# Seven products for eight over all eight input tiles of the up-projections of a two-block transformer kernel

## The reference

```python
def sq_relu_mlp(u, w_up, w_down):
    hdn = jax.nn.relu(u @ w_up)        # (1024, 1024) @ (1024, 4096)
    return (hdn * hdn) @ w_down        # (1024, 4096) @ (4096, 1024)
```

## Time and profile before

| | |
|---|---|
| median of 3 runs | 2346.39 us |
| the profiled execution | 2347.34 us, of which 2344.1 us is the span of its instructions |
| TensorE busy | 2322.2 us, 99% of the span, 11044 matmuls |
| VectorE (DVE), GpSimd (POOL), ScalarE (ACT) busy | 64%, 46%, 31% |
| DMA | 123.31 MB, 53 GB/s on average |

### The profile page before, as it was taken

How to read it: one execution, slowest core, us unless ns; L and a number is a source line. 1 busy time by engine, 2 the same in 40 slices (tenths; PEclk the granted TensorE clock), 3 DMA queues, 4 the chain that set the end, 5 groups by cost and what they waited for, 6 DMA issues and landing times.

```text
span 2344.1 us, 31876 instructions
## 1 busy us (share of the span) xinstructions
PE 2322.2 (99%) x11044; PEld 1939.3 (83%) x11044; DVE 1493.2 (64%) x2090; ACT 724.5 (31%) x1175; POOL 1084.9 (46%) x1218
## 2 busy tenths in 40 slices
PE   8999999999999999999999999999999999999997
PEld 6888888888888888888888888888888888888886
DVE  6666667756567666765566656554676676677434
ACT  4233333323434433343330002002343344333411
POOL 4332323334556565655443333544465565656432
PEclk9999999999999999999999999999999999999999
DMA  4111101022111112111112111111111111121112
GB/s 152 37 29 36 35 28 36 28 90 72 54 55 54 45 54 63 49 50 54 55 45 72 37 37 45 45 45 45 45 46 59 58 54 45 54 63 46 54 54 81
DMA packets 37525, 123.31 MB, mean 53 GB/s; under 512 B 4800, under 2 KB 5952, under 8 KB 37440
## 3 DMA queue, kind: packets, MB, share of 16 engines
q1 hardware_dynamic: 36432, 120.54, 16.7%
q10 hardware_dynamic: 1008, 1.62, 0.2%
HBM read 117.95 MB, written 4.19 MB: 52 GB/s over the span
## 4 chain that ended last, share of the span: by engine, by line
PE 96%; DVE 2%; DVEq 1%; issue 0%; DMA 0%; SPq 0%; ACT 0%
PE prod_ps L583 13%; PE prod_ps L585 13%; PE prod_ps L584 13%; PE prod_ps L842 6%; PE prod_ps L841 6%; PE prod_ps L840 6%; PE side_ps L842 5%; PE side_ps L841 5%; PE side_ps L840 5%; PE prod_ps L926 4%; PE prod_ps L925 4%; PE prod_ps L927 4%; PE side_ps L720 2%; PE side_ps L636 2%; PE side_ps L642 1%; PE side_ps L926 1%
## 5 line engine op out<-in xcount | busy, mean ns | idle before, releaser
L583 PE MATMUL prod_ps<-operand_hi,w_hi 128*128 128x512 f32 x1464 | 584.1, 399 | 4.9 <-DVE operand_lo L1183 2.8
L585 PE MATMUL prod_ps<-operand_hi,w_lo 128*128 128x512 f32 x1464 | 572.5, 391 | 0.0
L584 PE MATMUL prod_ps<-operand_lo,w_hi 128*128 128x512 f32 x1464 | 571.5, 390 | 0.0
L452 POOL CAST w_hi<-w_raw 128x1024 fp32r<-128x1024 f32 x86 | 92.4, 1074 | 701.3 <-PE prod_ps L585 680.4
L486 POOL TENSOR_TENSOR w_lo<-w_raw,w_hi 128x256 fp32r<-128x256 f32 x160 | 143.9, 918 | 405.8 <-ACT w_hi L2192 405.8
L456 POOL TENSOR_TENSOR w_lo<-w_raw,w_hi 128x256 fp32r<-128x256 f32 x344 | 327.3, 981 | 6.9
L583 PEld LDWEIGHTS prod_ps<-operand_hi,w_hi 128*128 128x128 f32 x1464 | 275.5, 188 | 63.6 <-issue 4.8
L585 PEld LDWEIGHTS prod_ps<-operand_hi,w_lo 128*128 128x128 f32 x1464 | 275.3, 188 | 58.8
L584 PEld LDWEIGHTS prod_ps<-operand_lo,w_hi 128*128 128x128 f32 x1464 | 275.9, 188 | 53.1
L925 PE MATMUL prod_ps<-operand_hi,w_hi 128*128 128x512 f32 x384 | 149.9, 390 | 0.0
L926 PE MATMUL prod_ps<-operand_lo,w_hi 128*128 128x512 f32 x384 | 149.8, 390 | 0.0
(11 more groups left out here) (308 smaller groups left out, 4844.3 us busy)
## 6 DMA issues: line engine op xcount, KB each, us to landing
w_raw<-stream SPq DMA_DIRECT2D x202, 512.0 KB, 3.5
x_in<-x_t SPq DMA_DIRECT2D x16, 256.0 KB, 6.1
x_res<-x_t SPq DMA_DIRECT2D x8, 512.0 KB, 4.6
out_t<-x_res SPq DMA_DIRECT2D x16, 256.0 KB, 2.1
w_raw<-stream SPq DMA_DIRECT2D x8, 128.0 KB, 4.8
masks_f<-masks SPq DMA_DIRECT2D x1, 896.0 KB, 7.9
ret_rows<-head_rows ACTq DMA_DIRECT2D x1, 512.0 KB, 3.7
ret_cos<-rope ACTq DMA_DIRECT2D x1, 512.0 KB, 4.5
```

The lines of the kernel that those rows point to most:

```text
L583: nc.tensor.matmul(into, w_h, a_h, start=(k == 0), stop=False)
L584: nc.tensor.matmul(into, w_h, a_l, start=False, stop=False)
L585: last = nc.tensor.matmul(into, w_l, a_h, start=False, stop=(k == KT - 1))
```

## The change

The up pairs (all but the first of each perceptron) use seven products for eight over all eight input tiles: tiles 4 to 7 get their own operands (`y_op`, with T1 to T4) and their own pair unit, in slot 1. Each of the seven products is then two wino halves, slot 0 by `x_op` and slot 1 by `y_op`. `upper` and its bank b_z go. The order in a pair becomes P1, P5, P6, P2, P7, P3, P4.

There is no room for T2, T3 and T4 of tiles 4 to 7, so they share their place with residual tiles 0 to 5 (`swapped`): the residual tiles are written to DRAM (`park_x`) and read back (`fetch_x`), and the operands are read again (`fetch_op`), in every group.

The weights of both slots are prepared before an up pair: `split_both` on GpSimd, `both_first_highs` and `both_last_highs` on ScalarE, and on DVE the sums of S3 and S4 of both slots stand ahead of the addition and Relu of c12. The core of the diff, shortened:

```diff
-                def up_pair(g, r, q, u, into, start=False, ...
+                def up_pair(g, r, q, u, into, both_split=True, new=False, behind_down=False, fetched=False, in_last=None):
...
+                    copied(g, r, 1)
+                    bank = b_u
+                    both(S2, T2, False, 3, y_wait=1).then_inc(up_prod, 1)
+                    bank = b_w
+                    both(A12, B21, True, None).then_inc(up_prod, 1)
+                    copied(g, r, 3)
...
+                def squares_late(g, r, u, h, b, then=None, between=None):
+                    act.wait_ge(evac, at(g, 16, 2 * (u0 + u) + 2))
+                    nc.scalar.activation(h[2], h[2], ACT.Square).then_inc(h_sq, 1)
+                    if then is not None:
+                        then(2)
+                    if between is not None:
+                        between()
+                    relu_copy(g, r, u, h, b)
+                    act.wait_ge(evac, at(g, 16, 2 * (u0 + u) + 4))
+                    nc.scalar.activation(h[1], h[1], ACT.Square).then_inc(h_sq, 1)
...
+                def both_last_highs(g, q, u):
+                    for slot in range(2):
+                        high_s34(slot, summed(g, q, 3 + slot))
+                    for slot in range(2):
+                        unit_free(g, u + slot)
+                        high_a22(slot)
...
-                    squares_early(g, 3, far_h)
-                    highs(g, 8, 12, 0)
-                    squares_late(g, 3, 10, far_h, far_banks)
+                    both_first_highs(g, 3, 11, 12)
+                    squares_early(g, 3, far_h)
+                    squares_late(g, 3, 10, far_h, far_banks, between=lambda: both_last_highs(g, 11, 12))
...
-                    finish_up(g, 3, 10, far_banks, far_h, before12=lambda: all_sums(g, 12, 0))
+                    finish_up(g, 3, 10, far_banks, far_h, sums_behind(g, 3, 12, 1),
+                              before12=lambda: more_sums_behind(g, 3), before11=sums_behind(g, 3, 12, 0))
...
+                finish_up(g, 3, 10, far_banks, plain_h(2), lambda: sum_then_lows(WINO_GROUPS - 1, 3, 12, 0, near_h),
+                          before21=lambda: more_sums_behind(WINO_GROUPS - 1, 3), before11=sums_behind(g, 3, 12, 0))
...
+                for op, m, half in ((B11, 4, 0), (B12, 4, 1), (B21, 6, 0)):
+                    for kk in range(2):
+                        part = nc.scalar.activation(y_raw[op][:, kk], x_res[:, m + kk, tokens(half)], ACT.Copy,
+                                                    scale=gain[:, gain_row, m + kk:m + kk + 1])
+                    part.then_inc(y_scaled, 1)
```

More of the change, by code:

```diff
@@ new lines, in up_pair, with half, both @@
+                def up_pair(g, r, q, u, into, both_split=True, new=False, behind_down=False, fetched=False, in_last=None):
+                    b_u, b_v, b_w = into[:3]
+                    u += u0
+                    def half(bank, slot, which, op, first, part, y_wait=None):
+                        if part is not None:
+                            if both_split:
+                                parts(g, q, 2 * part - 1 + slot)
+                            else:
+                                parts(g, q + slot, part)
+                        if slot and y_wait is not None:
+                            if new:
+                                pe.wait_ge(y_ready, 4 * index + (2, 1, 3, 4)[y_wait])
+                            elif fetched and y_wait:
+                                pe.wait_ge(op_back[y_wait - 1], at(g, 16, 16 * (first_group + 1)))
+                        return wino(bank, slot, which, (x_op, y_op)[slot][op], first and slot == 0)
+                    def both(*product, y_wait=None):
+                        half(bank, 0, *product)
+                        return half(bank, 1, *product, y_wait=y_wait)
+                    pe.wait_ge(evac, at(g, 16, 2 * u - 4))
@@ L944, in up_pair @@
                     if behind_down:
                         free(g, PAIRS - 2, "P4")
[L946 to L947 removed]
+                    half(b_u, 0, A11, B11, True, 1)
+                    if not new:
+                        half(b_u, 1, A11, B11, True, 1).then_inc(up_prod, 1)
                     pe.wait_ge(evac, at(g, 16, 2 * u - 2))
[L949 to L951 removed]
@@ L952, in up_pair @@
[L952 to L963, removed]
@@ L974, in up_pair @@
[L974 to L980, removed]
+                    half(b_v, 0, S1, T1, True, 2)
@@ new lines, in up_pair @@
+                    copied(g, r, 3)
+                    bank = b_u
+                    both(S3, T3, False, 4, y_wait=2).then_inc(up_prod, 1)
+                    copied(g, r, 2)
+                    bank = b_v
+                    both(S4, B22, False, None).then_inc(up_prod, 2)
+                    pe.wait_ge(up_taken, at(g, 2, first_up + r + 1))
+                    pe.wait_ge(w_split, at(g, 8, u + 1))
+                    half(b_u, 0, A22, T4, False, None).then_inc(prod, 2)
+                    if in_last is not None:
+                        in_last()
@@ L1576, in end_c12 @@
                     def end_c12():
-                        nc.vector.tensor_tensor(c12, b_v, c21 if not last else last_u2, ALU.add)
+                        nc.vector.tensor_tensor(c12, b_v, c21, ALU.add)
                         dve.drain()
```

480 lines of the change are left out of this document (355 added, 125 removed).

## The result

The changed kernel takes 2363.46 us (median of 4 runs, 2361.13 to 2364.0) against 2346.39: a ratio of 1.0066, 95% interval 1.0054 to 1.0079. It is slower by 17 us. The forecast was 2345, with a range up to 2362; the median lies 1.5 us outside it, and on the other side of no change than my likeliest case.

What follows compares the result with a forecast made beforehand. TensorE, busy 99% of the span, was taken to bound the kernel by its number of matmuls. Terms -41.2 + 19.2 + 13.6 + 4.8 + 1.6 = -2.0 us against 2347.34 gave 2345, range 2322 to 2362.

Steps and rivals of the forecast that it cites:

- my likeliest case: The prediction's own sum of terms, 2345 us with its own range 2335 to 2355, chance 0.50.
- Matmuls: Up pairs after each perceptron's first: 180 matmuls fewer on TensorE at 0.2273 us each, a gain of 40.9 us.
- Near wait: Near pairs: TensorE waits 1.6 us for ScalarE's first copy, 12 times, 19.2 us (bounds 1.0 to 2.2 each).
- Rival 1: S3/S4 sums on DVE wait in full for GpSimd, 1.5 to 3 us: +21, 2366 us, chance 0.12.
- Plain phases: Last two pairs of each perceptron: TensorE waits 3.4 us for the copy, 4 times, 13.6 us.
- Start: Start of each perceptron: six y_raw scalings ahead of copy 1, 2.4 us wait, twice, 4.8 us (2 to 7).
- Second pair: Second up pair of each perceptron: first copy late by 0.8 us, twice, 1.6 us (0 to 4).
- First plain product: Reordered plain product: saves the 0.17 us wait ahead of it, twice, a gain of 0.3 us.
- Rivals 2 and 3: 2: near wait absent because queues run down faster, 2326, chance 0.20; 3: all new waits hidden, 2306, chance 0.08.
- Transfers: Nine DMAs of 1 MB in each group, at most 7.0 us each, costed at nothing.
- rival 4: Transfers or weights late in SyncE's queue, delaying near pairs; 2 us in 12 groups gives 2369, chance 0.10.
- some 5 us of room: Slack claimed for the tightest transfer: residual tiles 0 and 1, fetched after P6 of the near pair, before DVE needs them.

Runs made afterwards that it cites:

- The kernel with all moves: Changed kernel with c12 ahead of the far-phase sums, copies ahead of start scalings, first plain units split early, plain low parts moved: 2315.31 us, ratio 0.9866.

## Why the prediction was wrong

The mechanism was right in kind: what is saved on TensorE is given back in waits for ScalarE's copy of P1, late because `relu_copy` stands behind a longer list. The forecast was 18 us too low, and the range 1.5. Step by step, each waiting term with its 0.27 included:

- **Matmuls**: 180, 40.9 us. Right.
- **Near wait**: 1.6 forecast, 17.1 / 12 + 0.27 = 1.7 measured; 20.3 for 19.2. Right, and the undoing of the sums' place gave 22.3 back. The copy ended some 7 us behind the pair's start, as worked out. The way there was only nearly right: `relu_copy` at 3.2 and not 3.6, and GpSimd, which I put beside all four sums, ran beside the first two only and was then idle for 3.74 us, since its next low parts wait for the S3 and S4 high parts. Rival 1, sums that wait in full for GpSimd, therefore fell: the four took 2.1 us, 0.5 more than alone, where it asked for 1.5 to 3. That its time, 2366, is near the measured one is luck.
- **Plain phases**: 13.6 forecast, 11.1 measured. Fair.
- **Start**: 4.8 forecast, 5.0 measured. Right.
- **Second pair**: 1.6 forecast, 3.8 measured, inside its own bounds (0 to 4), but by another hand. GpSimd's low part of the next unit ended the wait, not the copy.
- **First plain product**: forecast as a gain of 0.3, measured as a cost of 6.0. This is the first step that failed. I counted the 0.17 us of the earlier trace rows as saved, which they were, and put the product's first matmul at nothing. Before, TensorE was done with the slot of the first plain unit 24 matmuls ahead of the end of the last pair; after, 6. GpSimd's cast and low parts, 2.77 us of waiting, can't be fitted in there. In the row below GpSimd had waited 11.50 us for that slot. I had not asked, of a reordered product, when its weights' buffer comes free.

```profile
1152.97 1.04 POOL L552 CAST w_hi<-w_raw 128x1024 fp32r<-128x1024 f32 x1 [11.50 <-PE side_ps L967]
1154.10 2.78 POOL L556 TENSOR_TENSOR w_lo<-w_raw,w_hi 128x256 fp32r<-128x256 f32 x4
```

- **The clock**: no term at all, 8.6 measured. This is the second and larger step that failed. The sum took a stall as its own length. I had the waits of 2.2 and more in hand and did not ask what the granted clock does behind one. The kernel before with six more scalings carries it: of two equal waits the one with a fall behind it cost 4.1 us, the other 2.5. With the waits of the start gone, 8.0 us came back for 5.0 of waits. The 8.6 is what the profiled execution shows, with falls behind five of its eight waits; the number differs between executions.
- **Rivals 2 and 3**: fell, since the waits were there. As soon as c12 stands ahead the near wait is absent, as rival 2 had it, but by an edit and not by faster queues.
- **Transfers, and rival 4**: costed at nothing, and in the changed kernel no wait of TensorE names one. The kernel with all moves has the same transfers and gets 31 of the 40.9 us, so they cost at most a part of the other 9.8. But "some 5 us of room" was wrong as a figure: I had looked at the fetch of tiles 0 and 1, and the narrow place is a weight's load queued behind the parks. A second write of each park used that up and cost 64 us.

The two failed terms are 14.9 us (8.6 and 6.3), and the second pair adds 2.2; the plain phases were 2.5 too dear. Had I counted the first two, the sum would have been 2360. The upper bounds of my range came from waits alone, and no case of mine had a cost that a wait sets off elsewhere.

What is open: 2.5 us of the 18.1 between the spans; why of two equal waits, one in each perceptron, only one is followed by a fall of the clock; and the 4 us that separate the best version from the whole gain.

## What to carry to other kernels

Where a filled TensorE gets a new wait, price it twice: its idle and what the granted clock does behind it; twelve waits of 1.4 us cost no clock here, and of those of 2 us and more seven in ten did. When a list of an engine that is 34% busy gets longer, follow the one instruction that frees TensorE's bank, and place work that waits for another engine (here the sums) so that it overlaps with work that doesn't. When a product is moved or shortened, ask of every buffer when it comes free, who refills it and what is queued behind that refill: the moved high parts cost 43 us through a chain of four engines, and none of them was full.

## What the runs showed of the hardware

- In the perceptrons of the eleven kernels profiled here TensorE has 86 waits of 0.9 to 1.8 us, and behind none of them the granted clock fell. It has 86 of 1.96 us and more (up to 4.9), and behind 60 of these it fell, as often behind those of 2.2 us (the changed kernel: five of eight). No fall there stands without such a wait ahead of it. A wait of 2.2 us at 420 us, for the scores of the HGRN mixer, has none behind it in any of the eleven. A fall cost 1.6 us where it could be compared with an equal wait without one.
- A wait costs some 0.27 us more than the idle that the profile gives: 1.65 for 1.38, and 2.5 for 2.23 in the kernel before with six more scalings.
- Beside GpSimd, VectorE's four low parts took 4.97 us, where four alone took 2.49; two subtractions of GpSimd's took 1.43 while VectorE was idle and 3.40 beside its 1024-wide operations (723.77 to 728.65):

```profile
718.05 1.43 POOL L621 TENSOR_TENSOR w_lo<-w_s,w_hi 128x256 fp32r<-128x256 f32 x2 [3.74 <-ACT w_more_hi L2414]
...
724.17 3.40 POOL L621 TENSOR_TENSOR w_a_lo<-w_raw,w_more_hi 128x256 fp32r<-128x256 f32 x2
```

- 1 MB to DRAM took 8.0 us from issue to landing where 7.0 was my upper bound, worked out from the 512 KB loads; the same back took 6.6 and 5.1 (KB each, us to landing):

```profile
x_park<-x_res SPq DMA_DIRECT2D x42, 1024.0 KB, 8.0
x_res<-x_park SPq DMA_DIRECT2D x42, 1024.0 KB, 6.6
swapped<-op_park SPq DMA_DIRECT2D x36, 1024.0 KB, 5.1
```
